# A hybrid decoder step: input projection with the convolution's tiles first, all taps on VectorE in alternating channels, attention levels under v and g, rank product on column tiles

## The reference, cut to what matters

```python
z = h @ w_in                       # q, k (256 each), v, g (512 each), a_lr (16), u = ua, ug (512 each)
log_a = log_sigmoid(a_lr @ w_a2 + b_a) / TAU
o, s_new = gla_recurrence(q, k, v, log_a, s_gla)    # S_t = diag(a_t) S_{t-1} + k_t^T v_t, o_t = q_t S_t
o = standardize(o) * gla_norm_g * silu(g)
glu = ua * sigmoid(ug)
y = depthwise_conv(concat(conv_buf, glu), conv_w)   # width 31, 512 channels
y = silu(layer_norm(y + conv_b))
return concat(o, y) @ w_out, s_new, last 30 rows of the glu
```

## Time and profile before

| | us |
|---|---|
| median of 3 runs | 787.1 |
| the three runs | 786.85, 787.10, 789.83 |
| span of the profiled execution | 787.9 |
| PE busy | 708.9 |
| DVE busy | 282.2 |
| ACT busy | 229.9 |
| POOL busy | 120.1 |

### The profile page before, as it was taken

One profiled execution on the slowest core, in us unless ns is written; L12 is line 12 of the kernel. 1 busy time (PEld: TensorE's weight loads), 2 busy tenths in 40 slices (PEclk: granted clock), 3 DMA queues, 4 the chain that ended last, 5 costly groups with the idle time before them and its releaser, 6 DMA issues.

```text
span 787.9 us, 22105 instructions
## 1 busy us (share of the span) xinstructions
PE 708.9 (90%) x9481; PEld 461.2 (59%) x9485; DVE 282.2 (36%) x681; ACT 229.9 (29%) x415; POOL 120.1 (15%) x213
## 2 busy tenths in 40 slices
PE   3999999899899999977777988989999999989684
PEld 1678877577465565544444656756656565655342
DVE  1138999841652121211111266138212222112016
ACT  1234658520432212211111235025122222222113
POOL 0021487710011010100000000001101010101000
PEclk9999999789999999988899999999999999999987
DMA  9998963589995899999999999999799999999941
GB/s 310 391 344 249 321 216 107 180 287 355 394 417 214 334 427 426 424 422 429 422 421 427 413 381 388 406 410 418 308 426 428 420 428 426 419 427 424 421 203 55
DMA packets 66762, 282.00 MB, mean 358 GB/s; under 512 B 13709, under 2 KB 14419, under 8 KB 50294
## 3 DMA queue, kind: packets, MB, share of 16 engines
q1 hardware_dynamic: 64418, 274.05, 87.6%
q0 software_dynamic: 1600, 5.70, 2.2%
q10 hardware_dynamic: 676, 1.24, 0.5%
HBM read 278.54 MB, written 3.37 MB: 358 GB/s over the span
## 4 chain that ended last, share of the span: by engine, by line
PE 63%; DMA 19%; DVE 8%; SPq 5%; ACT 3%; issue 2%; DVEq 0%; ACTq 0%
PE bank L811 16%; DMA arena<-in_w_up 13%; PE bank L1091 7%; PE bank L820 7%; PE bank L790 6%; PE bank L849 5%; PE bank L953 5%; PE bank L649 5%; DMA arena<-in_w_gate 4%; DMA arena<-in_w_ada 3%; DVE t L1462 3%; SPq L509 1%; SPq L519 1%; PE bank L668 1%; DVE arena L1456 1%
## 5 line engine op out<-in xcount | busy, mean ns | idle before, releaser
L811 PE MATMUL bank<-arena 128*32 128x256 f32 x3136 | 193.7, 403 | 37.4 <-DMA arena<-in_w_up 29.7
L811 PEld LDWEIGHTS bank<-arena 128*32 128x32 f32 x3136 | 112.2, 116 | 111.9 <-issue 56.6
L1913 DVE SCALAR_TENSOR_TENSOR arena<-arena,bank 128x128 f32<-128x128 f32 x49 | 22.4, 456 | 304.4 <-ACT arena L1386 304.4
L820 PE MATMUL bank<-arena 128*32 128x256 f32 x1568 | 93.6, 379 | 0.0
L2046 POOL TENSOR_TENSOR arena<-t 128x192 f32<-128x192 f32 x51 | 26.4, 518 | 377.8 <-PE bank L790 377.7
L1389 ACT ACTIVATE arena<-bank 128x256 f32<-128x256 f32 x49 | 18.8, 383 | 199.7 <-PE bank L820 199.7
L790 PE MATMUL bank<-htm,arena 128*32 128x256 f32 x1224 | 75.8, 379 | 0.0
L953 PE MATMUL bank<-arena 128*128 128x264 f32 x320 | 73.9, 389 | 1.4 <-ACT arena L1230 1.4
L953 PEld LDWEIGHTS bank<-arena 128*128 128x128 f32 x320 | 59.9, 190 | 13.1 <-ACT arena L1230 1.6
L1386 ACT ACT_TABLE_LOAD x49 | 62.9, 1283 | 1.7 <-issue 0.8
L820 PEld LDWEIGHTS bank<-arena 128*32 128x32 f32 x1568 | 47.5, 110 | 25.1
(11 more groups left out here) (278 smaller groups left out, 642.6 us busy)
## 6 DMA issues: line engine op xcount, KB each, us to landing
arena<-in_w_down SPq DMA_DIRECT2D x32, 2048.0 KB, 24.4
arena<-in_w_ada SPq DMA_DIRECT2D x24, 2048.0 KB, 18.8
arena<-in_w_gate SPq DMA_DIRECT2D x22, 2048.0 KB, 24.5
arena<-in_w_up SPq DMA_DIRECT2D x44, 1024.0 KB, 21.7
arena<-in_w_up SPq DMA_DIRECT2D x10, 2048.0 KB, 19.7
arena<-in_w_gate SPq DMA_DIRECT2D x20, 1024.0 KB, 19.0
arena<-in_w_in_even SPq DMA_DIRECT2D x5, 2048.0 KB, 23.0
arena<-in_w_out_even SPq DMA_DIRECT2D x2, 2048.0 KB, 11.2
```

Of the source, the lines that this page charges most:

```text
L811: last = mm(GU[C * q:C * (q + 1), :].rearrange("p (a n) -> p a n", a=2), hgc[:, C * k:C * (k + 1)], cols, start=(k == 0), stop=(k == KD - ...
L820: last = mm(Y[C * dq:C * (dq + 1), :], hidt[:, C * q:C * (q + 1)], wd[:, q, 2 * P * dq:2 * P * (dq + 1)], start=(q == 0), stop=(q == 3), t ...
L1913: v.scalar_tensor_tensor(out=hid.rearrange("p (j i) -> p i j", j=KF), in0=columns(silu), scalar=tabs[:, bass.ds(NCH + g, 1)], in1=columns( ...
```

## The change

Everything changed lies between the opening and the output projection of layer 0.

- The tile order becomes `ug` 0, `alr`, `ua` 0, `la` 0 and 1, the other `ug` and `ua` pairs, then `qk`, then `v` and `g`. The first 15 tiles (`N_HEAD`) come before the levels; `v` and `g` go one to an iteration under the levels.
- `alr` is made in four column tiles of PE at once, as four partial sums on 4 x 32 partitions; `w_a2` is loaded four times and `la` contracts over all 128 partitions, which adds the partial sums.
- All 124 taps are on DVE. `taps(n, channels)` never takes the same channel tile twice in a row where another has taps left; 86 come before the levels, 38 in iterations 1 to 7. ACT and POOL have no taps.
- The decay of the samples' states moves to ACT (16 scalings), the update becomes 4 multiply-adds for two samples, through one bank (7).
- `ada` unit 4 and the history's sum come before `qk`, unit 5 into iteration 2. Turning and spreading v moves into iterations 5 to 8.
- `g`'s sigmoid is one instruction behind the levels, and POOL's gating one instruction.
- The norm stage is reordered: the convolution's sums go first, the attention's later.
- The fill order and slots follow the tile order, with the masks' transfer ahead of `v`.

The core of the diff:

```diff
-    plan = [(("ada", i), i) for i in range(4)]
-    plan += [(("in", n), s) for n, s in (("qk", 4), ("ug", 5), ("ua", 0), ("v", 1), ("g", 2))]
-    plan += [(("ada", 4), 3), (("ada", 5), 4), (("out0", 0), 5), (("out0", 1), 0)]
-    plan += [(("ada", 6 + i), s) for i, s in enumerate((1, 2, 3, 4))]
+    plan = [(("ada", i), s) for i, s in enumerate((0, 3, 4, 1))]
+    plan += [(("in", n), s) for n, s in (("ug", 2), ("ua", 5), ("qk", 0), ("v", 3), ("g", 4))]
+    plan += [(("ada", 4), 1), (("ada", 5), 2), (("out0", 0), 5), (("ada", 6), 1), (("out0", 1), 0)]
+    plan += [(("ada", 7 + i), s) for i, s in enumerate((2, 3, 4))]
...
-        Z_TILES = ([("alr", 0), ("qk", 0), ("la", 0), ("la", 1)] + [("qk", n) for n in range(1, 4)]
-                   + [(nm, n) for n in range(4) for nm in ("ug", "ua")] + [(nm, n) for nm in ("v", "g") for n in range(4)])
-        Z_BANK = [0, 1, 2, 3, 4, 5, 0] + [4 + i % 2 for i in range(16)]
+        Z_TILES = ([("ug", 0), ("alr", 0), ("ua", 0), ("la", 0), ("la", 1)] + [(nm, n) for n in range(1, 4) for nm in ("ug", "ua")]
+                   + [(nm, n) for nm in ("qk", "v", "g") for n in range(4)])
+        Z_BANK = [4, 0, 5, 1, 2, 3, 0, 4, 5, 1, 2, 3, 4, 5, 4, 5, 4, 5, 4, 5, 5, 5, 4]
+        N_HEAD = 15
...
                     for k in range(KD):
-                        pe.wait_ge(E("h0_ready"), k + 1)
-                        last = mm(o[0:16, 0:T], walr[:, k, :], h[:, k, :], start=(k == 0), stop=(k == KD - 1))
+                        r = C * (k % 4)
+                        last = mm(o[r:r + C, 0:T], walr[:, k, :], h[:, k, :], start=(k < 4), stop=(k >= 4),
+                                  tile_position=(0, r))
...
+            for s in range(1, LEVELS + 2):
+                if s == LEVELS + 1:
+                    pe.wait_ge(E("vtm_copied"), 2)
+                z_tile(N_HEAD - 1 + s)
+                if s == 7:
+                    spread_v(1)
+                if s == 8:
+                    spread_v(3)
+                level(s)
+                if s == 2:
+                    ada_unit(5, False)
+                if s == 5:
+                    z_free(pe, Z_TILES.index(("v", 3)))
+                    turn_v_samples()
+                    turn_v(0)
+                if s == 6:
+                    spread_v(0)
+                    turn_v(1)
+                if s == 7:
+                    spread_v(2)
...
+            def taps(n, channels):
+
+                for _ in range(n):
+                    fresh = [c for c in channels if left.count(c) < TAPS and left[-1:] != [c]] or [left[-1]]
+                    c = min(fresh, key=lambda c: (left.count(c), c))
+                    j = left.count(c)
+                    left.append(c)
...
+            def state_update(i):
+
+                dve.wait_ge(E("vb_done"), i + 1)
+                dve.wait_ge(E("state_decayed"), 4 * i + 4)
+                for bb in range(2):
+                    b = 2 * i + bb
+                    for a in range(2):
+                        old = state[:, b, DV * a:DV * (a + 1)]
+                        stt(old, bank[7][:, SEQ * bb + DV * a:SEQ * bb + DV * (a + 1)], k_[:, a, SEQ + b:SEQ + b + 1], old,
+                            ALU.mult, ALU.add, E("vb_taken") if bb and a else None)
...
+            taps(9, (0,))
...
+            gated(1)
+            S.sync()
+            taps(15, (0, 1))
+            gated(2)
+            S.sync()
+            taps(20, (0, 1, 2))
+            gated(3)
...
+            taps(24, (0, 1, 2, 3))
+            dve.wait_ge(*attended("hist_done"))
...
+            taps(17, (0, 1, 2, 3))
...
             for s in range(1, LEVELS + 2):
                 level_qk(s)
                 if s <= LEVELS:
                     level_diff(s + 1)
-                if 2 <= s < 2 + CC:
-                    gated(s - 2)
                 level_copy(s - 1)
...
+                if s <= LEVELS:
                     S.sync()
-                    taps(*[(0, 8, 16, 22, 27, 32, 37, 42)[s - 2 + i] for i in range(2)])
+                    taps(6 if s < 3 else 5 if s < LEVELS else 4 * TAPS - len(left), (0, 1, 2, 3))
+                if s == LEVELS:
+                    S.sync()
+                    S(v.memset(epsb[:, :], EPS), E("cn_r"))
+                    state_update(0)
+            for i in range(1, 4):
+                state_update(i)
             level_copy(LEVELS + 1)
```

More of the change, by code:

```diff
@@ L1065, in _ @@
-            pe.wait_ge(E("norm_sq"), 1)
-            partial_sums(bank[0][:, 0:T], t2, range(HEADS), None).then_inc(E("norm_sums"), 1)
-            pe.wait_ge(E("norm_sq"), 3)
-            partial_sums(bank[4][:, 0:T], t2[:, CC:], range(CC), None).then_inc(E("norm_sums"), 1)
+            pe.wait_ge(E("o_copied"), 2)
+            pe.wait_ge(E("kl_copied"), 1)
+            for i in range(2):
+                last = mm(bank[(1, 7)[i]][:, :], ones, t1[:, 2 * i:2 * i + 2, 0:SEQ], start=True, stop=True)
@@ new lines, in _ @@
+            A(fn(klp, klp, ACT.Exp), E("decay_act"))
+            z_tile(Z_TILES.index(("ug", 2)))
+            z_tile(Z_TILES.index(("ug", 3)))
+            act.wait_ge(s_state, 32)
+            act.wait_ge(E("decay_act"), 2)
+            for b in range(NS):
+                for a in range(2):
+                    A(fn(state[:, b, DV * a:DV * (a + 1)], state[:, b, DV * a:DV * (a + 1)], ACT.Identity,
+                         scale=asmp[:, a, b:b + 1]), E("state_decayed"))
+            ada_unit(4)
@@ L1264, in _, with turned_v @@
+            for i in range(Z_TILES.index(("qk", 0)), N_HEAD):
+                z_tile(i)
+            def turned_v(tt):
+                act.wait_ge(*attended(f"v_tr{tt}"))
+                copy(vtm[:, tt, :], bank[4][:, :], E("vtm_copied"))
             level_exp(1)
             for s in range(1, LEVELS + 2):
-                if s >= 2 and Z_BY[4 + 2 * s] == "a":
-                    z_tile(4 + 2 * s)
                 if s <= LEVELS:
                     level_exp(s + 1)
-                if s >= 4:
-                    taps(10 * (s - 4), 10 * (s - 4) + 5)
@@ L1283, in _ @@
-            taps(45, 55)
-            act.wait_ge(E("kl_ready"), 1)
+                z_tile(N_HEAD - 1 + s)
+                if s == 2:
+                    ada_unit(5)
+                if s == 5:
+                    act.wait_ge(*attended("vs_tr"))
+                    copy(vstm[0:NS, :], bank[7][0:NS, :], E("vs_copied"))
+                    turned_v(0)
+                if s == 6:
+                    turned_v(1)
+            A.sync()
+            A(fn(sg, sg, ACT.Sigmoid), E("g_sig"))
+            act.wait_ge(*summed("conv_sum"))
@@ new lines, in _ @@
+            gated(0)
+            for n in range(2):
+                i = Z_TILES.index(("la", n))
+                dve.wait_ge(E("z_done"), i + 1)
+                one_op(la[:, n, :], bank[Z_BANK[i]][:, 0:T], vec[:, V_BA + n:V_BA + n + 1], ALU.add, E("z_copied_d"))
+            S.sync()
+            one_op(la2, la, -1.0, ALU.mult)
+            S.sync()
+            tt(la2, la2, la, ALU.max, E("decay_dve"))
+            taps(9, (0,))
+            dve.wait_ge(E("decay_act"), 1)
+            stt(la, la, 0.0, la2, ALU.min, ALU.subtract)
@@ L1720, in _ @@
+            dve.wait_ge(*summed("conv_mean"))
+            for p in range(2):
+                c = slice(4 + 2 * p, 6 + 2 * p)
+                stt(t1[:, c, :], bank[5][:, 0:T].unsqueeze(1).broadcast_to([P, 2, T]), -1.0 / (C * FF), t1[:, c, :],
+                    ALU.mult, ALU.add, E("norm_c"))
+            dve.wait_ge(*summed("o_sums"))
             for i in range(2):
```

372 lines of the change are left out of this document (146 added, 226 removed).

## The result

| | before | after |
|---|---|---|
| median of the runs, us | 788.47 (4 runs, 786.85 to 790.86) | 806.7 (4 runs, 800.96 to 809.2) |
| span of the profiled execution, us | 787.9 | 799.1 |
| start of the output projection, us | 164.6 | 176.1 |
| DVE busy / POOL busy, us | 282.2 / 120.1 | 280.6 / 73.0 |

The changed kernel is slower: the recorded ratio is 1.019, with a 95% interval of 1.0147 to 1.0232. It is not the quotient of the two medians, which is 1.023. Of its four executions the profiled one is the fastest (800.96, span 799.1). The others have spans of 802.7, 806.9 and 807.4, and with them a mean PE clock of 0.950, 0.945 and 0.943 against 0.956. A run's time is 1.8 to 2.9 us above its span wherever the record of this study has both.

A forecast was written before the change was run, and what follows sets the result against it. PE was taken to bound the projection and levels before the change. Levels from 94.5, last tap 135.1, last level 147.0 and output projection 172.5 put it 7.9 us later than 164.6, so 795.0 us, range 787 to 804.

The forecast's parts named there:

- PE and DVE up to the levels: Before the levels: PE, waiting 4.5 us for ada unit 4, decides by 1.8 over DVE's 92.7; levels start at 94.5.
- What a tap costs: Taps on DVE: 0.40 us each when alternating channel tiles, 0.526 when chained; 124 taps cost 50.7 us.
- no overlap of taps: Rival for DVE's taps: alternation gives nothing, 0.526 for all, +20.6 us, 808; chance 0.06.
- The levels: Iterations 1 to 7: DVE sets the pace at 5.4 to 5.8 us each; last tap at 135.1.
- The exchange of iterations 7 and 8: From last tap to last level: a chain of PE and DVE through one bank, 11.9 us, to 147.0.
- The tail: Last level to output projection: serial PE work of 12.4 us, then the norm stage, 24.5, plus 1.0 for clock.
- the tail folds: Rival behind the last level: PE's 12.4 us run beside the norm stage, -6.3 us, 781; chance 0.12.
- Carrying the shift one to one: From output projection to the end: its shift from 164.6, 7.9 us, reaches the end in full.
- Near balance: Rival: taps at 0.33, full PE clock behind its wait, no loss on `g`: +2.5 us, 790; chance 0.22.

The follow-up runs named there:

- e4: The changed kernel with the taps of one channel tile after another instead of alternating: 812.54 us, ratio 1.0287 to the kernel before.
- e10: The changed kernel with ACT's first exponential of the level differences ahead of its qk copies: 803.9 us, ratio 1.0166 to the kernel before.
- e3: The changed kernel with idle products filling PE's waits before the second and third spreads of v: 803.08 us, ratio 1.0121 to the kernel before.
- e0: The changed kernel run once more, unaltered: 806.24 us, ratio 1.018 to the kernel before.
- e6: e2 with ada unit 4 and the first v tile between qk and level 0, and ACT's first exponential early: 789.42 us, ratio 0.9993 to the kernel before.
- e8: e7 with spread 3 and the turning of the keys behind the attention's output on PE: 786.83 us, ratio 0.995 to the kernel before.
- e7: e6 with the last takeover ahead of updates 1 to 3, keys turned behind the attention's output, square-root table early: 788.79 us, ratio 0.9979.
- e2: The changed kernel with the spreads of v alternating between two banks, two of them in iteration 6: 794.87 us, ratio 1.0031 to the kernel before.
- e9: e8 with six idle products on PE ahead of iteration 8's wait for ACT's copy of v: 785.21 us, ratio 0.9925 to the kernel before.

## Why the prediction was right on the side and short on the size

The forecast was slower, 795.0, with 787 to 804. The profiled execution took 800.96, the median was 806.7, which is above the range; the recorded ratio, 1.019 of the 787.1 from which the forecast was made, would be 802.0, inside it. So the direction was right and the forecast of 7.9 us took about half of the loss. Its four steps, by the profiled execution:

| step | predicted | measured |
|---|---|---|
| levels start | 94.5 | 94.8 |
| last tap ends | 135.1 | 137.2 |
| last tap to last level | 11.9 | 16.1 |
| last level to output projection | 25.5 | 22.8 |
| output projection | 172.5 | 176.1 |

The errors are 0.3, 1.8, 4.2 and, the other way, 2.7. So a part of the 3.6 us is luck: without the tail forecast too long the start would have been off by 6.3.

**PE and DVE up to the levels: right.** Ada unit 4 was the late one, with a wait of 6.04 where 4.5 was forecast (its transfer landed 0.7 later and the tiles ended 0.9 earlier), and half clock behind it. DVE's head ended at 91.1 (forecast 92.7).

**What a tap costs: right.** The pitch was 0.40, on 16 taps in a row, and 0.52 chained in e4. POOL's products for the history end at 66.2; the group at 64.97 takes 8.62 for 19 taps, against 7.7 at a pitch of 0.40, and the multiplication ahead of it 0.90 instead of 0.41. That is 1.4 us, where 1.5 was forecast. So the rival "no overlap of taps" is out. The Trainium skill's page "VectorE: DVE Perf Modes", section "The DRAIN you can't avoid", says that the next instruction waits until the pipeline is empty, and adds that one that is not held starts earlier. The chained taps fit the first; the alternating ones, 0.40 apart with a duration of 0.48, fit only the second.

**The levels: right in kind, 1.8 short.** DVE took 5.5 to 6.0 us per iteration (forecast 5.4 and 5.8). The missing term is the first exponential. ACT had its table load (1.28) and the activation (0.63) behind the last qk copy, and DVE waited 1.22 for them; e10 removes that wait. The other 0.6 is spread over the iterations, among it one gap of 0.47 ahead of a takeover. I had DVE's and PE's order at this point but not ACT's. The forecast that PE waits in each iteration was wrong in form: PE ran ahead at 4.95 each and paid once, 4.73 ahead of spread 1.

**The exchange of iterations 7 and 8: the step that failed in size.** The order of the chain was as forecast. I priced each of its PE pieces at full clock, spread 0.97, level 1.2, tile 3.66, and kept 1.0 for the clock in the tail. Measured were 1.48, 2.24, 1.97 and 5.20 for spread, level, spread and tile, 4.1 over their sum. A piece of PE's that stands behind a wait of 2 to 5 us had to be priced as the unit of the earlier trace rows was, at up to half clock, in the whole chain and not at the `g` tile alone. e3 shows it: with idle products in those waits the same chain takes 11.2 from spread 1 on, instead of 14.8 to 16.5.

**The tail: 2.7 too long in the forecast.** It was serial, as forecast, and far from the 15.4 at which "the tail folds" would have decided; the attention's squares were its last input, as I had said against that rival. 1.0 of the 2.7 was the `g` tile's clock, which lies in the exchange. The rest is PE's work: I had 12.4 and 10.6 less 0.9, so 22.1 us, taken from windows at clocks of 0.83 and 0.68, and it took 19.2 at 0.93.

**Carrying the shift one to one: right.** Output projection and span are apart by 623.3 before and 623.0 after; in the profiles of e0 to e10 that start lies between 160.8 and 186.0, and the distance stays between 621.5 and 624.4.

**What no step had: the spread of the clock.** By its profile the change costs 11.5 us up to the output projection, by the medians 18, and by those of e0 and the 25 runs beside it 15.9. The two first profiles understate it: that of the changed kernel is its fastest execution, 5.7 under its median, and that of the kernel before lies over its own (some 790 against 788.5). The other executions of the changed kernel ran with a lower mean clock. One of its slower ones was profiled, e0 (804.07), and lost 1.3 us in the exchange and 1.6 in the tail. The profiles of kernels that wait for ada unit 4 in the same place show what this can look like: about 4 us more in history and qk, in four of seven. That the changed kernel's own slowest executions, 808 to 809, lost it there is argued, not shown, since none of them was profiled.

**Near balance** (790) asked for taps at 0.33 and full clock behind the wait; neither came. That e6 lands at 789.4 says something else: the new order itself is neutral. Its losses were mainly two placements, one bank for four spreads (11.4 by the medians) and a unit ahead of its weights (7.8), with the late exponential behind them (2 to 3); these overlap, since their sum is over the 16 us of the loss. With PE's and DVE's order in the tail put in step as well (e8) it is 0.5% faster than before.

## What to carry to other kernels

When work moves off the path of one engine, look for a single buffer that makes two engines take turns behind it: here a second PSUM bank, with the spreads placed accordingly, was worth 11 us, more than the order of the taps (6.5) and the faster rank product (0) together. Price every PE instruction behind a wait at both clock levels, along the whole chain; in e8 the `g` tile took 5.51 behind a wait of only 0.69. When two engines hand work to each other, change both written orders together: e7 moved the takeover up on DVE and left spread 3 in front of the output on PE, and its output began no earlier than e6's (141.09 and 140.35) until e8 moved the spread.

## What the runs showed of the hardware

- Two multiply-adds of 128x256 on DVE with different outputs start 0.40 us apart where each takes 0.48; on the same output 0.52 (17 in 6.81 and in 8.82 us).
- How long the half clock lasts behind a wait is not the same from one execution to the next: the `g` tile took 5.20 and 6.79 in two executions of one program, the history's sum 1.95 or 3.58 behind the same wait and unit (e2 and e3 differ only further down).
- Idle products kept the clock at 1.00 through 16 us with a wait of 0.87 in them (e3). The short filler of e9 brought the `g` tile to full clock (3.72 for 5.51), cost 2.76, and did nothing for the next stretch: the samples' output (4.76) and the sums behind it (3.78) ran at a granted clock of 0.76 and 0.50, much as in e8 (4.43 and 3.78), though PE had worked at 1.00 with waits of only 0.27 and 0.24 us in the 6 us before.
